# Output units of a fused attention and MoE block ordered by column halves, its LayerNorm's last step moved off VectorE

## The chip, the cores and the metric

The kernel runs on one core of a Trainium2 chip. The metric is the device time of one launch in microseconds (us), lower is better; three runs of a kernel give a median. Engines are named TensorE (PE), VectorE (DVE), ScalarE (ACT), GpSimd (POOL) and SyncE (SP), whose queue issues the large transfers.

## What is computed

One encoder block over 512 tokens of width 1024 in fp32: two attention mixers (a sliding window one and a sparse one), a gated merge, the projection `w_out`, a LayerNorm, a routed mixture of experts, a second LayerNorm.

```python
m = sigmoid(ga) * (oa @ w_branch_a) + sigmoid(gb) * (ob @ w_branch_b)
h = layernorm(ALPHA * x + m @ w_out, ln1_g, ln1_b)      # (x - mean) * rstd * g + b
# router: top-1 of 4 groups, then top-2 of its 8 experts, per token
y = sum over chosen experts of ((silu(h @ w_gate) * (h @ w_up)) * weight) @ w_down
out = layernorm(ALPHA * h + y, ln2_g, ln2_b)
```

## The kernel before

The program is written out by hand for each engine, with semaphores between them; the order in a block's text is the order on that engine. Tokens are four tiles of 128 (`TT` = 4). The stages are the input projections and attention, the branch products, the out stage, the expert loop and the tail. The change touches the out stage and how it hands over to the expert loop.

**Out stage.** `m @ w_out` is split in high and low parts, three matmuls for each of 8 row blocks `k`. A unit `("out", i)` is one token tile times one half of the 1024 columns: 24 matmuls into one PSUM bank (`bank_of`, L126). Before, unit `2t + h` is tile `t`, half `h`, so a tile's two halves follow each other. DVE takes a unit out of PSUM with `residual(t, h)` (L1766), which adds it to the scaled input rows in `h1` and sums the row; `centre(t)` (L1776) makes the mean and writes `z = (h1 - mean) * g`; ACT makes the sum of squares (`squares`, L1504), POOL the variance and `rstd` (L761, L764); `norm1(t)` (L1790) writes `h1 = z * rstd + b`, again on DVE, in two halves with the columns reordered (`row_half`, `in_half`), and signals `h1_ready`.

PE turns `z` (`turn_z`, L1082), ACT copies it to `h1T` (`copy_h1t`, L1511), PE multiplies by the router weights (`router`, L1093), DVE finds group and experts (`select`, L1799, and `weigh`, L1823), PE counts ranks in each expert (`rank`, L1104), and DVE makes the selection of rows from these (`place`, L1833). PE's order around this is L1143 to L1163, DVE's is L1855 to L1865:

```python
for t in range(TT):                # DVE before
    residual(t, 0)
    if t:
        select(t - 1); weigh(t - 1); place(t - 1)
    residual(t, 1); centre(t); norm1(t)
select(TT - 1); place(TT - 1)
```

After the last unit PE gathers the rows of experts 0 and 1 by matmul with the selection (`picked_rows`, L1115), makes the table of tokens of every expert (L1168), turns the picked rows (L1130), and starts expert 0. The rows of later experts are gathered from `h1_dram` by POOL (L772, L782), which waits until all four tiles of `h1` are stored there by SP (L626).

**Expert loop.** 32 experts of 3 MB of weights each (gate, up, down: 1 MB each, L564, L568, L581) pass through six slots of SBUF (`EXS`, `ex_off`). Per expert PE does L1229 (gate and up), L1211, L1130 and L1245 (down). A slot's gate and up are loaded again when PE is done with them (`refill_gate_up`, L634, waits `gu_done`; `refill_down`, L639, waits `d_done`). Slots 3, 4 and 5 lie over memory that the out stage still reads: slot 3's gate and up are the left columns of `w_o_lo`, slot 5 reaches into the merged input. So SP (L610 to L632) loads slots 0 to 2 before the out units, and the other 9 MB as the out stage lets go of its memory. SP issues in order: a wait for `h1_ready` ahead of a load holds that load too.

## Time and profile before

| | us |
|---|---|
| median of 3 runs (lowest, highest) | 757.41 (757.24, 758.32) |
| the profiled execution | 759.57 |
| its span, first to last instruction | 757.8 |
| PE busy | 731.0 (96%) |
| DVE, ACT, POOL busy | 376.3, 303.5, 255.4 |
| DMA over the span | 161.00 MB, 212 GB/s |

All times inside the kernel are counted from the span's start. The page's strip of 40 slices has about 19 us each; a line of the timeline gives start, duration, engine, source line, operation, output and inputs, a count where equal neighbours are merged, and in brackets the engine's idle time before it with the one that ended it. The out stage runs from 436.8 to 490, the hand-over to 503.2, the expert loop to 730.6.

### The profile page before, as it was taken

What the parts mean: (1) busy time and instruction counts of PE and PEld (TensorE: products, weight loads), DVE (VectorE), ACT (ScalarE), POOL (GpSimd) and SP (SyncE); (2) the same over time, 40 slices, a digit from 0 to 9 for tenths busy, and PEclk for the clock granted to TensorE, in tenths of its full rate; (3) what the DMA queues carried; (4) which work ended last, traced back from release to release, by engine and by line L of the source; (5) the groups of instructions that cost most, each with busy time, mean ns of one, the idle gap of its engine ahead of it and who ended that gap; (6) DMA issues with size and microseconds to landing.
All of it is one profiled execution on the core that took longest, in us unless ns stands there. A gap on an engine that the chain in (4) does not pass through costs nothing.

```text
span 757.8 us, 12102 instructions
## 1 busy us (share of the span) xinstructions
PE 731.0 (96%) x4400; PEld 511.3 (67%) x4400; DVE 376.3 (50%) x1001; ACT 303.5 (40%) x614; POOL 255.4 (34%) x310
## 2 busy tenths in 40 slices
PE   7999999999999999999999999999999999997894
PEld 6965886777777777778888878754555555554442
DVE  2436998877678867664222256645511111111146
ACT  5346325777556665565232141223322222221123
POOL 4721542222222222225695200023323333333211
PEclk9999999999999999999999999999999999999998
DMA  8511242222222222224631384699999999999973
GB/s 234 168 56 56 86 138 70 70 71 70 70 70 70 70 70 70 70 70 167 222 110 63 134 360 195 231 402 413 417 413 418 417 417 417 417 416 418 412 300 155
DMA packets 60199, 161.00 MB, mean 212 GB/s; under 512 B 8666, under 2 KB 37346, under 8 KB 48116
## 3 DMA queue, kind: packets, MB, share of 16 engines
q1 hardware_dynamic: 55108, 152.31, 53.4%
q0 software_dynamic: 5040, 8.02, 2.9%
q8 instruction: 31, 0.51, 0.3%
q14 instruction: 20, 0.16, 0.1%
HBM read 152.56 MB, written 16.25 MB: 223 GB/s over the span
## 4 chain that ended last, share of the span: by engine, by line
PE 85%; DMA 6%; DVE 3%; ACT 2%; issue 2%; POOL 1%; SPq 1%; DVEq 0%; POOLq 0%; ACTq 0%
PE psum L924 38%; PE psum L1229 12%; PE psum L1245 6%; PE psum L910 6%; PE psum L999 4%; DMA arena<-in_w_up_dram 4%; PE psum L1057 3%; PE psum L1130 2%; PE psum L1035 2%; PE psum L1051 2%; PE psum L852 1%; PE psum L969 1%; PE psum L1211 1%; DMA arena<-pair_rows 1%; PE psum L1100 1%
## 5 line engine op out<-in xcount | busy, mean ns | idle before, releaser
L924 PE MATMUL psum<-arena,arena 128*128 128x512 f32 (+1 forms) x1296 | 315.1, 394 | 0.2 <-POOL arena L709 0.2
L924 PEld LDWEIGHTS psum<-arena,arena 128*128 128x128 f32 x1296 | 235.6, 188 | 58.9 <-issue 14.1
L709 POOL TENSOR_TENSOR arena<-arena,arena 128x256 fp32r<-128x256 f32 (+1 forms) x138 | 138.1, 1035 | 234.3 <-ACT arena L1339 234.3
L1229 PE MATMUL psum<-arena,gate_a_T 128*64 128x256 f32 x1024 | 123.4, 383 | 6.9 <-DMA arena<-in_w_up_dram 6.7
L1229 PEld LDWEIGHTS psum<-arena,gate_a_T 128*64 128x64 f32 x1024 | 70.8, 137 | 55.0 <-issue 25.8
L1339 ACT ACTIVATE arena<-arena 128x2048 fp32r<-128x2048 f32 x27 | 51.5, 1907 | 37.1 <-DMA arena<-in_w_branch_b_dram 24.9
L1995 DVE COPY gate_a_T<-psum 128x128 f32<-128x128 f32 x32 | 9.3, 291 | 114.3 <-PE psum L1211 114.3
L1442 ACT ACTIVATE arena<-psum 128x1024 f32<-128x1024 f32 (+3 forms) x48 | 37.1, 773 | 67.6 <-PE psum L1035 48.4
L1432 ACT ACTIVATE arena<-arena,negm 128x193 f32<-128x193 f32 (+5 forms) x128 | 62.4, 492 | 3.6 <-DVE negm L1700 3.6
L1245 PE MATMUL psum<-arena,gate_a_T 128*64 128x512 f32 x256 | 61.9, 604 | 0.4 <-DVE gate_a_T L1995 0.4
L1550 ACT ACTIVATE gate_a_T<-psum 64x256 f32<-64x256 f32 x32 | 12.1, 377 | 117.5 <-PE psum L1229 117.5
L1989 DVE SCALAR_TENSOR_TENSOR gate_a_T<-gate_a_T,psum 64x256 f32<-64x256 f32 x32 | 13.3, 415 | 58.5 <-ACT gate_a_T L1550 58.3
L1699 DVE TENSOR_REDUCE mx<-arena 128x4 f32<-128x772 f32 (+5 forms) x48 | 40.5, 843 | 1.6
L1710 DVE TENSOR_SCALAR arena<-arena,mx 128x192 f32<-128x192 f32 (+4 forms) x128 | 40.3, 368 | 1.7
L794 POOL DMA_INDIRECT pair_rows<-gate_a_T,idx x30 | 30.9, 1029 | 30.3 <-ACT gate_a_T L1561 30.3
L910 PE MATMUL psum<-arena,arena 128*128 128x512 f32 x128 | 40.5, 398 | 0.4 <-DVE merged_low L1740 0.4
L782 POOL DMA_INDIRECT arena<-h_rows,idx x30 | 31.5, 1049 | 25.6 <-POOL idx L779 25.6
L1695 DVE SCALAR_TENSOR_TENSOR arena<-arena,psum 128x128 f32<-128x128 f32 (+3 forms) x64 | 28.2, 482 | 21.3 <-PE psum L999 21.3
L779 POOL COPY idx<-tok_i 128x1 int32 (+1 forms) x30 | 5.6, 185 | 85.8 <-PE psum L1130 85.8
L1561 ACT ACTIVATE gate_a_T<-psum 128x512 f32<-128x512 f32 x30 | 17.9, 597 | 39.4 <-PE psum L1245 39.4
L999 PE MATMUL psum<-arena,arena 64*128 64x192 f32 (+4 forms) x256 | 33.3, 389 | 0.0
L1245 PEld LDWEIGHTS psum<-arena,gate_a_T 128*64 128x64 f32 x256 | 15.7, 136 | 22.5 <-issue 18.2
(258 smaller groups left out, 881.9 us busy)
## 6 DMA issues: line engine op xcount, KB each, us to landing
arena<-in_w_down_dram SPq DMA_DIRECT2D x32, 1024.0 KB, 20.8
arena<-in_w_gate_dram SPq DMA_DIRECT2D x31, 1024.0 KB, 13.6
arena<-in_w_up_dram SPq DMA_DIRECT2D x31, 1024.0 KB, 17.7
arena<-in_w_in_dram SPq DMA_DIRECT2D x19, 1024.0 KB, 5.5
pair_rows<-arena SPq DMA_DIRECT2D x16, 256.0 KB, 5.7
arena<-in_w_branch_a_dram SPq DMA_DIRECT2D x4, 1024.0 KB, 5.8
arena<-in_w_branch_b_dram SPq DMA_DIRECT2D x4, 1024.0 KB, 5.2
arena<-in_w_out_dram SPq DMA_DIRECT2D x4, 1024.0 KB, 8.1
```

Of the source, the lines that this page charges most:

```text
L709: nc.gpsimd.tensor_tensor(lo[:, k], raw[:, k], hi[:, k], ALU.subtract).then_inc(w_split, DT // n)
L782: pool.indirect_dma_start(out=xg[s], out_offset=None, in_=h1_dram, in_offset=bass.IndirectOffsetOnAxis(ap=idx[:, s:s + 1], axis=0), bounds ...
L910: ins = nc.tensor.matmul(ps, mp, wp, start=k == 0 and p == 0, stop=k == DT - 1 and p == 2)
L924: ins = nc.tensor.matmul(ps[:, columns(kind)], wp[:, k, col:col + P], xp[:, k, columns(kind)], start=k == 0 and p == 0, stop=k == DT - 1 a ...
L999: ins = nc.tensor.matmul(psum[:, 2 * (n % 2) + par, 256 * i:256 * i + w], q, k, start=True, stop=True)
L1229: ins = nc.tensor.matmul(psum[CAP * g:CAP * g + CAP, 2 + s % 2, 0:FF], xgT[s % 2][:, k % 4, k // 4, :], ex_gu[slot][:, g, k, :], start=k = ...
L1245: ins = nc.tensor.matmul(psum[CAP * half:CAP * half + CAP, 4 + s % 2, :], hidT[s % 2][:, k, :], ex_d[slot][:, k, 512 * half:512 * half + 5 ...
L1339: nc.scalar.activation(w_hi[c % RING], w_raw[c % RING], ACT.Copy).then_inc(w_high, 1)
L1432: ins = nc.scalar.activation(out, src, ACT.Exp, bias=negm[:, n % 4, h:h + 1], accum_out=den[:, n % 4, h:h + 1])
L1442: nc.scalar.activation(pt_sb[n % 2][:, 0:cols], psum[:, 4:6, :].rearrange("p b c -> p (b c)")[:, 0:cols], ACT.Copy).then_inc(pt_copied, 1)
L1699: step(V.tensor_reduce(mx[:, n % 4, 0:heads], s[:, :, w0:] if kind == "A" else s, AX.X, ALU.max))
L1710: ins = V.tensor_scalar(part, part, mx[:, n % 4, h:h + 1], None, ALU.mult)
```

## The change

1. **Order of the units.** Unit `TT * h + t` is tile `t`, half `h`: the four left halves come first, then the four right halves. The last one shares bank 4 with the first right half. `residual` of the left half of tile 3 is taken late (`TAKEN_IN`), since its `h1` rows lie over merged input that unit 6 still reads.
2. **SP.** Once the four left halves are done, slot 3's gate and up and slot 4's down are loaded. Then come the stores of `h1` tiles 0, 1 and 2, each behind its `h1_ready`; then, behind `wo_front_read` and the last unit, the 5 MB of slot 3's down, slot 5 and slot 4's gate; then the store of tile 3 and slot 4's up.
3. **LayerNorm's last step.** `norm1` is gone from DVE. ACT does `h1 = z * rstd` in two instructions behind the copies of `h1T` (`scale_z`), and POOL adds `b` in two instructions (128x512 each) before it signals `h1_ready`. `centre(t)` waits for `z_scaled` and no longer for `h1_ready`.
4. **PE and DVE order.** `rank(t)` comes a tile later; `router(2)` stands behind the last unit; `place(2)` stands behind `select(3)`, and `rank(2)` has a bank of its own.

```diff
@@ -90,7 +90,7 @@
         out += [("b", 2 * i + j, 21 + 2 * i, 128 * j) for j in range(2)]
-    out += [("out", 2 * t + i, None, 512 * i) for t in range(TT) for i in range(2)]
+    out += [("out", TT * i + t, None, 512 * i) for i in range(2) for t in range(TT)]
     return out
@@ -118,6 +118,9 @@
+TAKEN_IN = [0, 1, 2, 4, 5, 6, 3, 7]
+
+
 def columns(kind):
@@ -126,7 +129,7 @@
     if kind == "out":
-        return 4 + i % 4
+        return 4 if i == 2 * TT - 1 else 4 + i % TT
     if kind in "ab":
@@ -424,6 +427,7 @@
+        RANK_BANK = [3, 3, 6, 3]
@@ -473,8 +477,8 @@
             elif kind == "out":
-                if UNITS[u][1] >= 4:
-                    eng.wait_ge(r_ready, UNITS[u][1] - 3)
+                if UNITS[u][1] >= TT:
+                    eng.wait_ge(r_ready, TAKEN_IN.index(UNITS[before[-1]][1]) + 1)
             elif before:
@@ -611,25 +615,28 @@
             expert(2, 2)
+            sp.wait_ge(unit_done, UNIT["out", TT - 1] + 1)
+            gate_up(3, 3)
+            down(4, 4)
             for t in range(TT):
-                if t == TT - 2:
-                    sp.wait_ge(unit_done, UNIT["out", 2 * t + 1] + 1)
-                    residual_rows(TT - 1)
                 if t == TT - 1:
-                    sp.wait_ge(unit_done, UNIT["out", 6] + 1)
-                    gate_up(3, 3)
-                    down(4, 4)
-                    sp.wait_ge(unit_done, UNIT["out", 7] + 1)
+                    sp.wait_ge(wo_front_read, 1)
+                    down(3, 3)
+                    up(5, 5)
+                    sp.wait_ge(unit_done, UNIT["out", 2 * TT - 1] + 1)
                     gate(4, 4)
-                    down(3, 3)
+                    gate(5, 5)
+                    down(5, 5)
                 sp.wait_ge(h1_ready, t + 1)
...
                              ).then_inc(h1_stored, 16)
+                if t == TT - 3:
+                    sp.wait_ge(unit_done, UNIT["out", 2 * TT - 2] + 1)
+                    residual_rows(TT - 1)
             for rows, row in ((ln2g, ln2_g), (ln2b, ln2_b)):
...
             up(4, 4)
-            expert(5, 5)
@@ -763,6 +770,11 @@
                                         ).then_inc(rstd_ready, 1)
+                pool.wait_ge(z_scaled, 2 * t + 2)
+                for h in range(2):
+                    rows = row_half(h1[:, t, :], h)
+                    ins = nc.gpsimd.tensor_tensor(rows, rows, in_half(ln1b, h), ALU.add)
+                ins.then_inc(h1_ready, 1)
             pool.wait_ge(h1_stored, 16 * TT)
@@ -893,7 +905,7 @@
                 if kind == "out":
-                    t = i // 2
+                    t = i % TT
                     tok = slice(t * P, (t + 1) * P)
@@ -908,6 +920,8 @@
                             ins = nc.tensor.matmul(ps, mp, wp, start=k == 0 and p == 0, stop=k == DT - 1 and p == 2)
+                        if i == 2 * TT - 1 and k == DT // 2 - 1:
+                            ins.then_inc(wo_front_read, 1)
                     if k1 == DT:
@@ -1104,18 +1118,20 @@
-                if t:
-                    pe.wait_ge(ranks_taken, t)
+                if t == TT - 2:
+                    pe.wait_ge(r_ready, TAKEN_IN.index(2 * TT - 2) + 1)
+                elif t:
+                    pe.wait_ge(ranks_taken, min(t, TT - 2))
                 for v in range(t + 1):
                     pe.wait_ge(oh_ready, v + 1)
-                    ins = nc.tensor.matmul(psum[:, 3, 0:NE], (upper_h if v == t else ones_h)[:, :],
+                    ins = nc.tensor.matmul(psum[:, RANK_BANK[t], 0:NE], (upper_h if v == t else ones_h)[:, :],
                                            oh_both[:, v, :], start=v == 0, stop=v == t)
...
                 if t == 0:
-                    pe.wait_ge(r_ready, 5 + e)
+                    pe.wait_ge(r_ready, TAKEN_IN.index(2 * TT - 1 if e == 0 else TT + e) + 1)
                 pe.wait_ge(h1_ready, t + 1)
@@ -1142,24 +1158,28 @@
             for k0, k1 in ((0, BACK), (BACK, DT)):
-                for h in range(2):
-                    unit(UNIT["out", h], k0, k1)
+                for t in range(2):
+                    unit(UNIT["out", t], k0, k1)
+            for u in range(2, TT + 1):
+                unit(UNIT["out", u])
             for t in range(1, TT):
-                unit(UNIT["out", 2 * t], 0, 4)
+                u = UNIT["out", TT + t]
+                unit(u, 0, 4)
                 turn_z(t - 1)
-                unit(UNIT["out", 2 * t], 4, DT)
+                unit(u, 4, 6)
+                if t >= 2:
+                    rank(t - 2)
+                unit(u, 6, DT)
                 router(t - 1)
-                unit(UNIT["out", 2 * t + 1], 0, 6)
-                rank(t - 1)
-                unit(UNIT["out", 2 * t + 1], 6, DT)
+            turn_z(TT - 1)
             picked_rows(0, 0)
+            router(TT - 1)
             picked_rows(0, 1)
-            turn_z(TT - 1)
-            router(TT - 1)
-            picked_rows(0, 2)
+            rank(TT - 2)
             picked_rows(1, 0)
...
             picked_rows(1, 1)
+            picked_rows(0, 2)
             picked_rows(0, TT - 1)
@@ -1517,11 +1537,19 @@
+            def scale_z(t):
+
+                act.wait_ge(rstd_ready, t + 1)
+                for h in range(2):
+                    nc.scalar.activation(row_half(h1[:, t, :], h), in_half(z, h), ACT.Copy, scale=ln[:, 0, 4, t:t + 1]
+                                         ).then_inc(z_scaled, 1)
+
             for t in range(TT):
...
                 copy_h1t(t)
+                scale_z(t)
                 if t == TT - 2:
@@ -1765,7 +1793,7 @@
-                u = UNIT["out", 2 * t + h]
+                u = UNIT["out", TT * h + t]
                 cols = slice(h * D // 2, (h + 1) * D // 2)
@@ -1775,26 +1803,17 @@
-                dve.wait_ge(r_ready, 2 * t + 2)
+                dve.wait_ge(r_ready, TAKEN_IN.index(TT + t) + 1)
                 V.tensor_scalar(ln[:, 0, 1, t:t + 1], ln[:, 0, 0, t:t + 1], ln[:, 0, 5, t:t + 1], -1.0 / D, ALU.add,
...
                     dve.wait_ge(h1t_done, 2 * t)
-                    dve.wait_ge(h1_ready, t)
+                    dve.wait_ge(z_scaled, 2 * t)
                 for h in range(2):
...
                                            ALU.add, ALU.mult).then_inc(z_ready, 1)
-
-            def norm1(t):
-
-                dve.wait_ge(rstd_ready, t + 1)
-                dve.wait_ge(z_ready, 2 * t + 2)
-                for h in range(2):
-                    ins = V.scalar_tensor_tensor(row_half(h1[:, t, :], h), in_half(z, h), ln[:, 0, 4, t:t + 1],
-                                                 in_half(ln1b, h), ALU.mult, ALU.add)
-                ins.then_inc(h1_ready, 1)
@@ -1834,7 +1853,7 @@
                 dve.wait_ge(ranked, t + 1)
-                rank = psum[:, 3, 0:NE]
+                rank = psum[:, RANK_BANK[t], 0:NE]
                 step(V.scalar_tensor_tensor(sel_code[:, t, :], rank[:, 0:PEX], 1.0, oh_both[:, t, 0:PEX], ALU.add,
@@ -1852,16 +1871,20 @@
             step(V.tensor_scalar(dst_shift[:, :], tokid[:, 0:1], CAP + 0.5, -1.0, ALU.is_gt, ALU.add))
+            for t in range(TT - 1):
+                residual(t, 0)
             for t in range(TT):
-                residual(t, 0)
+                if t == TT - 1:
+                    residual(t, 0)
+                residual(t, 1)
+                centre(t)
                 if t:
...
                     weigh(t - 1)
+                if 0 < t < TT - 1:
                     place(t - 1)
-                residual(t, 1)
-                centre(t)
-                norm1(t)
             select(TT - 1)
+            place(TT - 2)
             place(TT - 1)
```


**DVE, from the last residual to the table of tokens.** `arena_105` is `h1`, `arena_107` is `z`; `L1773`/`L1801` residual, `L1787`/`L1815` centre, `L1795` norm1, `L1804`/`L1823` the first instruction of `select`, `L1829`/`L1848` the last of `weigh`, `L1838`/`L1857` to `L1847`/`L1866` `place`, `L1870`/`L1893` behind the table. Before:

```order
L1773 SCALAR_TENSOR_TENSOR arena_105,ln<-psum,arena_105 128x512
L1779 TENSOR_SCALAR ln<-ln 128x1
L1787 SCALAR_TENSOR_TENSOR arena_107<-arena_105,ln,arena_94 128x512 x2
L1795 SCALAR_TENSOR_TENSOR arena_105<-arena_107,ln,arena_95 128x512 x2
L1804 SCALAR_TENSOR_TENSOR strip<-psum,ln,const 128x40
...
L1821 TENSOR_SCALAR arena_150<-arena_148,dst_code 128x2x32
L1838 SCALAR_TENSOR_TENSOR sel_code<-psum,arena_149 128x2
...
L1847 TENSOR_TENSOR in_slot<-col_s,ranks 128x2x64
L1870 TENSOR_SCALAR strip<-psum 128x32
```

With the change:

```order
L1801 SCALAR_TENSOR_TENSOR arena_105,ln<-psum,arena_105 128x512 x2
L1807 TENSOR_SCALAR ln<-ln 128x1
L1815 SCALAR_TENSOR_TENSOR arena_107<-arena_105,ln,arena_94 128x512 x2
L1823 SCALAR_TENSOR_TENSOR strip<-psum,ln,const 128x40
...
L1848 TENSOR_TENSOR md<-best 128x1
L1823 SCALAR_TENSOR_TENSOR strip<-psum,ln,const 128x40
...
L1857 SCALAR_TENSOR_TENSOR sel_code<-psum,arena_149 128x2
...
L1866 TENSOR_TENSOR in_slot<-col_s,ranks 128x2x64
L1857 SCALAR_TENSOR_TENSOR sel_code<-psum,arena_149 128x2
...
L1866 TENSOR_TENSOR in_slot<-col_s,ranks 128x2x64
L1893 TENSOR_SCALAR strip<-psum 128x32
```

The two instructions of norm1 are gone; a whole `select` and `weigh` (of tile 2) and a whole `place` now stand between the last residual and the table, beside those of tile 3.

**PE, from the last out unit to the table** (`L1122`/`L1138` picked rows, `L1089`/`L1103` turn_z, `L1100`/`L1114` router, `L1111`/`L1127` rank, `L1168`/`L1188` the table, `L1130`/`L1146` turning the rows). Before:

```order
L1122 MATMUL psum<-arena_105,arena_158 64x512 x4
L1089 MATMUL psum<-ident,arena_107 128x128 x8
L1100 MATMUL psum<-rw,arena_106 128x40 x8
L1122 MATMUL psum<-arena_105,arena_158 64x512 x4
L1111 MATMUL psum<-arena_149,ones_h 128x32 x3
L1111 MATMUL psum<-arena_149,upper_h 128x32
L1122 MATMUL psum<-arena_105,arena_158 64x512 x4
L1168 MATMUL psum<-arena_150,in_slot 64x32 x16
L1130 MATMUL psum<-ident,arena_108 128x128 x4
L1122 MATMUL psum<-arena_105,arena_158 64x512 x4
```

With the change (its first two rows follow the last matmul of the last unit):

```order
L1114 MATMUL psum<-rw,arena_106 128x40 x8
L1103 MATMUL psum<-ident,arena_107 128x128 x8
L1138 MATMUL psum<-arena_105,arena_158 64x512 x2
L1114 MATMUL psum<-rw,arena_106 128x40 x8
L1138 MATMUL psum<-arena_105,arena_158 64x512 x2
L1127 MATMUL psum<-arena_149,ones_h 128x32 x2
L1127 MATMUL psum<-arena_149,upper_h 128x32
L1138 MATMUL psum<-arena_105,arena_158 64x512 x2
L1127 MATMUL psum<-arena_149,ones_h 128x32 x3
L1127 MATMUL psum<-arena_149,upper_h 128x32
L1138 MATMUL psum<-arena_105,arena_158 64x512 x6
L1188 MATMUL psum<-arena_150,in_slot 64x32 x16
```

A second router product has come behind the last unit and ahead of turn_z; two picked rows (a pair is two matmuls) stand on either side of the router, and the third for expert 0 now follows the last rank.

**SP's queue, from the first store of `h1`** (`h_rows<-arena_105`; arena_114, 115, 116 are gate and up of slots 3, 4, 5, arena_120, 121, 122 down of slots 3, 4, 5). Before:

```order
L626 DMA h_rows<-arena_105 128x1024 x2
L605 DMA arena_105<-in_x_dram 128x1024
L626 DMA h_rows<-arena_105 128x1024
L564 DMA arena_114<-in_w_gate_dram 128x2048
L568 DMA arena_114<-in_w_up_dram 128x2048
L581 DMA arena_121<-in_w_down_dram 128x2048
L564 DMA arena_115<-in_w_gate_dram 128x2048
L581 DMA arena_120<-in_w_down_dram 128x2048
L626 DMA h_rows<-arena_105 128x1024
L629 DMA arena_94<-in_ln_g_dram 1x1024
L629 DMA arena_95<-in_ln_b_dram 1x1024
L568 DMA arena_115<-in_w_up_dram 128x2048
```

With the change:

```order
L568 DMA arena_114<-in_w_gate_dram 128x2048
L572 DMA arena_114<-in_w_up_dram 128x2048
L585 DMA arena_121<-in_w_down_dram 128x2048
L631 DMA h_rows<-arena_105 128x1024 x2
L609 DMA arena_105<-in_x_dram 128x1024
L631 DMA h_rows<-arena_105 128x1024
L585 DMA arena_120<-in_w_down_dram 128x2048
L572 DMA arena_116<-in_w_up_dram 128x2048
L568 DMA arena_115<-in_w_gate_dram 128x2048
L568 DMA arena_116<-in_w_gate_dram 128x2048
L585 DMA arena_122<-in_w_down_dram 128x2048
L631 DMA h_rows<-arena_105 128x1024
```

Three loads now stand ahead of the stores, and five loads stand between the stores of tiles 2 and 3.

## Rows read from the trace of the kernel before

**Rows 1.** The page's strip of 40 slices: DMA busy tenths, and GB/s.
```profile
DMA  8511242222222222224631384699999999999973
GB/s 234 168 56 56 86 138 70 70 71 70 70 70 70 70 70 70 70 70 167 222 110 63 134 360 195 231 402 413 417 413 418 417 417 417 417 416 418 412 300 155
```
**Rows 2.** What PE waited for, 500 to 730 us: total, times, longest.
```profile
PE psum L1229 <- DMA arena<-in_w_up_dram: 6.7, 5, 1.6
```
**Rows 3.** Windows: length, busy time of PE, PEld, DVE, ACT, POOL, PE clock, DMA share, GB/s.
```profile
465.00:479.00 14.00, 14.00 (x77) 11.76 (x76) 8.81 (x35) 2.33 (x4) 0.87 (x4) 1.00 0.20 75
...
500.00:520.00 20.00, 19.49 (x171) 11.78 (x169) 8.89 (x34) 5.22 (x12) 5.90 (x8) 1.00 1.01 415
...
700.00:720.00 20.00, 17.64 (x129) 9.55 (x126) 2.55 (x7) 3.43 (x7) 5.76 (x9) 1.00 1.02 413
```
**Rows 4.** Timeline of SP's queue: first of the late loads, last, first refill.
```profile
482.63 0.33 SPq L564 DMA_DIRECT2D arena<-in_w_gate_dram  x1
...
498.04 0.52 SPq L581 DMA_DIRECT2D arena<-in_w_down_dram  x1
506.83 0.33 SPq L564 DMA_DIRECT2D arena<-in_w_gate_dram  x1
```
**Rows 5.** Packets of SP's queue, 482.6 to 506.83 us: count, MB, share of engines.
```profile
q1 hardware_dynamic: 1363, 9.18, 98.6%
```
**Rows 6.** POOL's gathers: the page's queue line, and the first gather's instruction.
```profile
q0 software_dynamic: 5040, 8.02, 2.9%
```
```profile
502.49 1.30 POOL L772 DMA_INDIRECT arena<-h_rows,tok_i  x1 [9.21 <-DMA h_rows<-arena]
```
**Rows 7.** Windows behind the load issued at 436.95, DMA idle before: last column GB/s.
```profile
437.00:437.50 0.50, 0.50 (x4) 0.42 (x3) 0.50 (x1) 0.50 (x2) 0.00 (x0) 1.00 0.00 0
437.50:438.00 0.50, 0.50 (x4) 0.32 (x2) 0.50 (x2) 0.50 (x2) 0.00 (x0) 1.00 0.81 115
...
439.00:439.50 0.50, 0.50 (x4) 0.41 (x3) 0.50 (x2) 0.50 (x2) 0.00 (x0) 1.00 1.01 426
```
**Rows 8.** Timeline of PE: router of tile 2, last unit, what follows, expert 0.
```profile
482.44 1.87 PE L1100 MATMUL psum<-rw,arena 128*128 128x40 f32 x16
484.14 0.71 PE L910 MATMUL psum<-arena,arena 128*128 128x512 f32 x2
...
489.99 1.94 PE L1122 MATMUL psum<-arena,arena 128*64 128x512 f32 x8
...
503.16 3.62 PE L1229 MATMUL psum<-arena,gate_a_T 128*64 128x256 f32 x32
```
**Rows 9.** Timeline of DVE: select, weigh, place of tile 2; residual to place of tile 3.
```profile
484.35 0.26 DVE L1804 SCALAR_TENSOR_TENSOR strip<-psum,ln,const 128x40 f32<-128x40 f32 x1 [0.94 <-PE psum L1100]
...
487.75 0.15 DVE L1829 TENSOR_TENSOR md<-best 128x1 f32<-128x1 f32 x1
488.72 0.16 DVE L1838 SCALAR_TENSOR_TENSOR sel_code<-psum,arena 128x2 f32<-128x2 f32 x1 [0.81 <-PE psum L1111]
...
490.09 0.69 DVE L1773 SCALAR_TENSOR_TENSOR arena<-psum,arena 128x512 f32<-128x512 f32 x1
...
491.08 1.42 DVE L1787 SCALAR_TENSOR_TENSOR arena<-arena,ln,arena 128x512 f32<-128x512 f32 x2
...
495.37 0.26 DVE L1804 SCALAR_TENSOR_TENSOR strip<-psum,ln,const 128x40 f32<-128x40 f32 x1 [0.64 <-PE psum L1100]
...
499.38 0.29 DVE L1847 TENSOR_TENSOR in_slot<-col_s,ranks 128x128 f16<-128x128 f32 x1
```
**Rows 10.** Groups by form: an ACT copy of 128x512 inside SBUF.
```profile
L1458 ACT ACTIVATE arena<-arena 128x512 fp32r<-128x512 f32 x16 | 9.2, 618 | 0.0
```
**Rows 11.** Timelines: two POOL instructions of 128x1024, and a DVE one beside them.
```profile
384.61 4.77 POOL L750 TENSOR_TENSOR arena<-arena,arena 128x1024 fp32r<-128x1024 f32 x2
```
```profile
388.72 1.21 DVE L1755 TENSOR_TENSOR gate_a_T<-gate_a_T,arena 128x512 f32<-128x512 f32 x1
```
**Rows 12.** One line's instructions: durations in ns, least, median, most.
```profile
L1755 DVE TENSOR_TENSOR gate_a_T<-gate_a_T,arena x8: 684/799/1205, 367.0 to 438.8; 128x512 f32<-128x512 f32 x8
```
```profile
L1700 DVE TENSOR_SCALAR negm<-mx x48: 168/170/735, 112.5 to 335.4; 128x2 f32<-128x2 f32 x32, 128x4 f32<-128x4 f32 x16
```
```profile
L704 POOL TENSOR_TENSOR arena<-arena,arena x1: 3362/3362/3362, 19.1 to 19.1; 128x1024 fp32r<-128x1024 f32 x1
```

4 lines of the change are left out of this document (2 added, 2 removed).

## The prediction

> **What bounds the kernel now.** I read the strip of 40 slices first. The DMA moves 412 to 418 GB/s in nearly every slice from the 27th to the 38th, and only 70 in most slices of the first half [rows 1]. So the expert loop looks bound by its transfers, although PE is busy 96% of the span. The waits say the same: from 500 to 730 us PE waits for weights only five times, 6.7 us in all [rows 2], and the windows show the DMA full at both ends of the loop, while it is nearly idle at 465 to 479 us [rows 3]. PE starts the loop with six slots full of weights and is ahead of the transfers until it has used them up; then it takes a weight when it lands. From there on the end depends on one thing: when the unbroken stream of refills began.
>
> The queue's timeline gives that moment. SP issues the late loads from 482.63 to 498.04, and the first refill at 506.83, when PE has finished expert 0's gate and up [rows 4]. The late loads are 9 MB of weights (9 x 1.049 = 9.44) and a store (0.52), 9.96 MB; SP's queue had moved 9.18 of it by 506.83 [rows 5]. So 0.78 MB was left, and 0.26 MB of two gathers (8.02 MB in 63 of them, 0.13 each, the first issued at 502.49 [rows 6]): 1.04 MB, which at 417 GB/s is 2.5 us. The refills' bytes began at about 509.3, with no gap before them. How much of the cover a gap would need follows from a load issued while the DMA was idle: issued at 436.95, nothing moved before 437.5, 115 GB/s then, and the full rate only at 439.0 [rows 7]. Against full flow that is about 1.6 us lost (estimate, from these windows).
>
> The Trainium skill (DMA: Bandwidth & Descriptors, "Anatomy of one DMA — SWDGE (gpsimd) path") puts most of the fixed 2 us at the end of a transfer, in the receipt of the write, so almost nothing would be lost at the start. The rows differ for this queue; by the page the stream would begin at 511.2, and the sum below would come to 759.3 in place of 760.9.
>
> **What sets the start of expert 0.** It starts at 503.16. PE ends the last unit with router(2) ahead of it: router 482.44 to 484.14, unit to 489.99 [rows 8]. On DVE, tile 2's select and weigh take 484.35 to 487.90, its place 488.72 to 490.09 (1.37); then come residual(3,1), z from 491.08 to 492.50, select(3) at 495.37, and the last place ends at 499.67 [rows 9]. The table of tokens and the turned rows follow on PE. So the chain after the out units is DVE's, and whatever is put into it moves the start.
>
> **The change, part by part.**
>
> 1. *Units by halves, router(2) behind the last unit.* The last unit ends 1.7 us earlier, near 488.2. DVE cannot use all of it: between the rank that comes 18 matmuls into that unit (about 1.4 us before its end) and residual(3,1) it now does place(1), 1.37, and residual(3,0), 0.7. residual(3,1) starts near 489.0, 1.1 earlier, and z ends near 491.4.
>
> 2. *What stands behind it.* Before, tile 2's select, weigh and place were done ahead of residual(3,1). Now select(2) and weigh(2) (487.90 - 484.35 = 3.55) come behind z(3): to 494.95. select(3) takes 495.37 to 499.67 less its place of 1.37, so some 3.0: to 498.0. Then place(2) and place(3), 1.37 each: 500.7 against 499.67, +1.0. One more pair of picked rows behind the last rank: 0.2 (eight 128x512 matmuls took 1.94 [rows 8]; two at 0.24 stand there more, half of it beside DVE). Without anything on POOL, expert 0 starts **1.2 later**. Taking norm1 off DVE gives the chain nothing at tile 3: before, two of it (1.4 us) lay in the wait between z's end at 492.50 and select's start at 495.37 while PE turned z. At tiles 0 to 2 DVE waits for PE's units anyway.
>
> 3. *ACT.* Two scalings a tile, as long as the copy of 128x512 inside SBUF, 0.62 [rows 10], behind the copies of h1T, which PE's router reads. It lies beside PE: nothing. If it came ahead, it would cost the router 1.2.
>
> 4. *POOL.* Two adds of 128x512 a tile. Two adds of 128x1024 took 4.77, so one here is about 1.2 and a pair 2.4. A DVE instruction beside them, with two inputs in SBUF, took 1.21 where the same line mostly takes 0.8 [rows 11, 12]; a tiny one (two elements a row) that mostly takes 0.17 took 0.74 once [rows 12]. Both look like an instruction that waits until POOL's ends. Tile 2's pair falls beside place(1) and the residuals, tile 3's beside select(2), weigh(2) and select(3): both on the chain. A pair costs DVE between 0 (it only meets the residuals, which read PSUM) and 2.4 (DVE stands still for all of it). I take 1.6, two thirds, since the chain there is mostly of small instructions with SBUF inputs but some get in between: +3.2 for two pairs. Tiles 0 and 1 have their pairs under the units: nothing.
>
> The Trainium skill (SBUF — State Buffer, "Who interferes with whom") says that GpSimd and VectorE share a pair of ports as an exclusive lock: a VectorE operation with two SBUF inputs, or in a two-port mode, stands still until the other's instruction is over. The two rows agree in kind. By that rule both pairs would be lost whole, 4.9 in place of 3.2, and the time would be 762.6.
>
> So expert 0 starts 4.4 us later (bounds 1.2 and 6.1), near 507.6.
>
> 5. *SP.* Three loads go out about 20 us earlier, near 461, into a time when the DMA is idle [rows 3]. The other five stand behind the stores of h1, each of which waits for its `h1_ready`; that of tile 2 comes only when POOL has added, near 490.0 (z(2) turned by 485.4, copies and scalings 2.4, adds 2.4). So 0.52 + 5.24 + 0.52 + 1.05 = 7.3 MB go out from 491.6 on and land by 509.4 at 417 GB/s. That is ahead of the first refill, now at 506.83 + 4.4 = 511.2, whose bytes flow at 512.8. The DMA stands idle for some 3 us that it did not before. The refill stream begins 512.8 - 509.3 = **3.5 us later**, and so does every weight behind it. The 3 MB that came early buy nothing, because the slots are full and no further load may go out until PE frees one. PE's waits at the end get shorter by the difference: 6.7 + 3.5 - 4.4 = 5.8.
>
> **The sum.** 759.57 + 3.5 = 763.1 for the profiled execution. That one stood 2.2 above the median of 757.41, so the median comes to **760.9**. A measurement of this kernel can tell about 0.2%, 1.5 us, from no change.
>
> **The rivals.**
>
> - *No contention.* POOL's adds meet only residuals and waits. The start is 1.2 later, the refill is issued at 508.0 and flows at 509.6, just behind the prefill's 509.4: the stream moves by 0.3, and up to 0.7 with some blocking. Time 757.7 to 758.1, taken as 757.9. For it: most durations of L1755 are at its median. Against: its longest and L1700's. Chance 0.22.
> - *The early loads pay (the other side).* If the loop's end hangs on how many bytes are in SBUF when PE starts, and the refill is not the gate, then 3 MB more in hand take away all five waits, 6.7, and PE's own pace sets the end: 757.4 - 6.7 + 1.2 = 751.9. It decides if the queue behind the first refill was more than 2.5 us long, which rows 5 speak against: what the early loads relieve is only that backlog. Chance 0.09.
> - *POOL is slower.* The adds read `b` in reordered columns. The one 128x1024 instruction at the start of the kernel took 3.36 [rows 12], 1.7 for half. Two pairs that block in full are 6.8, the start moves 8.0 and the stream 7.1: 764.5. Chance 0.13.
> - That the change doesn't do what it says: the early loads may not go out early. They stand ahead of every `h1_ready` wait now, and depend on the fourth left unit alone, so I give this no chance of its own; since they buy nothing, the sum would be the same unless the five late ones were later still.
>
> **The numbers.** Forecast 0.56, the others as above. The range goes from 757.2 (no contention, less half a microsecond for the medians) to 764.0, which takes in the forecast's upper bound of 762.6 and the part of the slow case with a little less blocking. Below it lies the second rival, above it most of the third. Faster by over 0.2% 0.09, within it 0.22 (the first rival), slower 0.69.
>
> **What would show it.** Last unit ending near 488.2; place(3) ending near 504 and expert 0 at 507.6; DVE instructions of select, weigh or place several times their usual length beside POOL's adds of 1.2; three loads issued near 461 and five near 490; DMA near idle from 470 to 490 and for about 3 us ahead of a first refill at 511; PE's waits for weights 5.8 in all. The prediction is wrong if the first refill is issued later and the end does not move with it, or if DVE is not held up by POOL, or if the chain after the last unit is not DVE's: a wait of PE for `h1_ready` of tile 3 would show that.

## The result, and the profile after

| us | before | changed |
|---|---|---|
| median (lowest, highest), 7 runs each | 757.64 (757.24, 758.86) | 760.56 (759.43, 761.65) |
| profiled execution, its span | 759.57, 757.8 | 761.18, 759.3 |
| PE busy | 731.0 | 734.7 |
| POOL, ACT busy | 255.4, 303.5 | 266.4, 308.6 |

The changed kernel is slower: ratio 1.0036, 95% interval 1.0024 to 1.0047, 2.9 us between the medians. The forecast was 760.9.

**Where the two traces line up.** The spans differ by only 1.5 us where the medians differ by 2.9, since the profiled execution of before is 1.9 above its median and that of the changed kernel 0.6. Part of this may lie at its start, where the clock of before's trace was low (mean clock 0.994; 45 of the 59 executions of before beside the experiments have 0.996 or 0.997). From the windows of before, PE clock in the third column from the right:

```profile
8.00:10.00 2.00, 1.67 (x8) 1.47 (x8) 0.00 (x0) 0.61 (x2) 0.00 (x0) 0.62 1.00 346
10.00:12.00 2.00, 1.56 (x5) 1.21 (x5) 0.69 (x1) 1.02 (x2) 0.82 (x1) 0.52 1.07 390
```

It is not the whole of it: the changed kernel's trace comes to the out stage 0.3 later still. So from here on places are also counted from the out stage's first matmul: 436.76 in before, 437.08 in the changed kernel, written as +66.4 and the like. And how late the transfers run is taken from their bytes: what the DMA moved in the 285 us from that matmul on. Before and changed:

```profile
DMA packets 19525, 110.01 MB, mean 386 GB/s; under 512 B 4345, under 2 KB 4345, under 8 KB 7631
```
```profile
DMA packets 19269, 108.82 MB, mean 382 GB/s; under 512 B 4293, under 2 KB 4293, under 8 KB 7466
```

1.19 MB less, at 0.417 MB a us, is a stream **2.9 us late**, as much as the medians differ. A second measure is the place of the last expert's down product, which follows the last weights:

```profile
728.70 1.94 PE L1245 MATMUL psum<-arena,gate_a_T 128*64 128x512 f32 x8 [0.40 <-DVE gate_a_T L1995]
```
```profile
730.40 1.94 PE L1265 MATMUL psum<-arena,gate_a_T 128*64 128x512 f32 x8 [0.41 <-DVE gate_a_T L2018]
```

That is +291.94 and +293.32, **1.4 us late** only. Why the two measures differ by 1.4 is not known; twelve of the thirteen kernels compared with this one trace of before show a difference of 0.9 to 1.8, so a good part of it is likely to be that trace's own. The time itself is read from the medians; the places in a trace say where it is lost, to about a microsecond.

The strip of slices and the waits of PE from 500 to 730 us in the changed kernel, against [rows 1] and [rows 2]:

```profile
DMA  8511242222222222224632397399999999999984
GB/s 235 166 56 55 87 138 70 70 71 70 70 70 70 70 70 70 70 70 167 222 110 73 123 375 294 126 366 413 400 409 419 416 418 417 417 416 418 412 319 174
```
```profile
PE psum L1249 <- DMA arena<-in_w_up_dram: 4.8, 4, 1.5
...
PE psum L1146 <- DMA arena<-h_rows,tok_i: 0.9, 1, 0.9
```

The early loads show in the 25th slice (294 for 195), the hole before the late ones in the 26th (126 for 231). PE waits less for weights, and has a new wait: for the gathered rows of expert 2.

SP's queue, against [rows 4]:

```profile
459.95 0.33 SPq L568 DMA_DIRECT2D arena<-in_w_gate_dram  x1
...
490.09 0.32 SPq L631 DMA_DIRECT2D h_rows<-arena  x1
490.46 0.43 SPq L585 DMA_DIRECT2D arena<-in_w_down_dram  x1
...
497.66 0.33 SPq L631 DMA_DIRECT2D h_rows<-arena  x1
...
509.79 0.35 SPq L568 DMA_DIRECT2D arena<-in_w_gate_dram  x1
```

The late loads and the first refill go out as forecast in kind, and the windows around that refill show the gap (before had 412 GB/s over all of 506 to 512):

```profile
510.00:511.00 1.00, 1.00 (x24) 0.88 (x22) 0.66 (x2) 0.71 (x2) 0.69 (x2) 1.00 0.52 74
511.00:512.00 1.00, 0.82 (x9) 0.70 (x10) 0.17 (x1) 0.06 (x1) 0.70 (x2) 1.00 0.62 205
```

PE behind the last unit, against [rows 8]:

```profile
488.18 1.87 PE L1114 MATMUL psum<-rw,arena 128*128 128x40 f32 x16
491.25 1.95 PE L1103 MATMUL psum<-ident,arena 128*128 128x128 f32 x8 [1.20 <-DVE arena L1815]
493.13 1.85 PE L1138 MATMUL psum<-arena,arena 128*64 128x512 f32 x4
494.91 1.98 PE L1114 MATMUL psum<-rw,arena 128*128 128x40 f32 x16
...
506.12 3.62 PE L1249 MATMUL psum<-arena,gate_a_T 128*64 128x256 f32 x32
```

and the windows of the same stretch:

```profile
490.00:491.00 1.00, 0.05 (x1) 0.00 (x0) 0.93 (x4) 0.50 (x1) 0.07 (x1) 1.00 0.12 49
491.00:492.00 1.00, 0.75 (x4) 0.75 (x5) 1.00 (x3) 0.74 (x2) 0.17 (x1) 0.65 1.12 401
492.00:493.00 1.00, 1.00 (x6) 0.80 (x4) 0.83 (x7) 0.56 (x1) 0.57 (x2) 0.50 0.96 246
493.00:494.00 1.00, 1.00 (x3) 0.30 (x4) 0.86 (x7) 0.80 (x3) 0.00 (x0) 0.50 1.00 352
494.00:495.00 1.00, 1.00 (x5) 0.10 (x1) 0.90 (x6) 1.00 (x2) 0.00 (x0) 0.64 0.94 385
```

PE stood idle for 1.2 us, waiting for z of tile 3, and then ran at half rate (1.2 GHz for 2.4) for some 3.4 us. Four records of picked rows (two matmuls of the program, which leave two records each) took 1.85 there and 1.08 at full clock. The other executions of the changed kernel have a mean clock of 0.990 to 0.995, where before mostly has 0.996 or 0.997; a stretch of 3.4 us at half rate is 0.002 of the mean (estimate), so most of them are likely to have one.

DVE, against [rows 9]:

```profile
488.05 0.88 DVE L1866 TENSOR_TENSOR in_slot<-col_s,ranks 128x128 f16<-128x128 f32 x1
...
490.44 1.42 DVE L1815 SCALAR_TENSOR_TENSOR arena<-arena,ln,arena 128x512 f32<-128x512 f32 x2
...
495.17 1.26 DVE L1848 TENSOR_TENSOR md<-best 128x1 f32<-128x1 f32 x1
497.09 0.26 DVE L1823 SCALAR_TENSOR_TENSOR strip<-psum,ln,const 128x40 f32<-128x40 f32 x1 [0.67 <-PE psum L1114]
...
502.35 0.29 DVE L1866 TENSOR_TENSOR in_slot<-col_s,ranks 128x128 f16<-128x128 f32 x1
```

Counted from the out stage's first matmul, the start of expert 0 came from +66.40 to +69.04. Its pieces, each from start to start unless said:

| piece | before | changed | difference |
|---|---|---|---|
| first matmul to z(3) | 54.32 | 53.36 | -0.96 |
| z(3) to select(3) | 4.29 | 6.65 | +2.36 |
| select(3) to the last place's end | 4.30 | 5.55 | +1.25 |
| to expert 0 | 3.49 | 3.48 | 0 |

From place(1) on, two DVE instructions were held up by POOL's adds: 0.88 for 0.29, and 1.26 for 0.15. The second cost nothing: select(3) behind it waited for PE's router anyway. POOL's adds took 1.26 to 1.32 each.

The change's order of work does not always run so. Two of the kernels below, e3_all_late and e8_split_refill, have the same program on PE and DVE up to expert 0 and differ from it in their loads. In their traces PE waited the same 1.19 us for z and its clock stayed at 1.00; two instructions of weigh(2) were held, 1.32 for 0.24 and 1.33 for 0.37, and DVE went into select(3) without a wait; then PE waited 2.04 for its rank, the clock fell behind that, and expert 0 started at +70.5. From e8_split_refill:

```profile
489.84 1.32 PE L1106 MATMUL psum<-ident,arena 128*128 128x128 f32 x8 [1.19 <-DVE arena L1822]
```
```profile
493.07 1.32 DVE L1847 TENSOR_SCALAR arena<-arena,dst_code 128x64 f16<-128x64 f16 x1
494.43 1.33 DVE L1852 TENSOR_SCALAR arena<-arena,dst_code 128x32 f16<-128x32 f16 x2
```

So a start read from one trace of this order stands for itself to about 1.5 us.

### The profile page after: what moved, and what is told of

It reads as the page before. It is cut to its first block, busy times and chain, and to the rows that moved or that the text cites. A ratio compares the mean times of both kernels' runs of the same rounds, so it can differ in the third digit from the quotient of the medians.

```text
span 759.3 us, 12105 instructions
## 1 busy us (share of the span) xinstructions
PE 734.7 (97%) x4400; PEld 513.9 (68%) x4400; DVE 375.2 (49%) x993; ACT 308.6 (41%) x622; POOL 266.4 (35%) x318
## 4 chain that ended last, share of the span: by engine, by line
PE 80%; DMA 9%; SPq 3%; DVE 3%; issue 2%; POOL 2%; ACT 2%; DVEq 0%; POOLq 0%
PE psum L938 38%; PE psum L1249 10%; PE psum L922 5%; PE psum L1265 5%; PE psum L1013 4%; DMA arena<-in_w_up_dram 4%; PE psum L1071 3%; PE psum L1049 2%; PE psum L1146 2%; PE psum L1065 2%; PE psum L864 1%; DMA h_rows<-arena 1%; PE psum L983 1%; DMA arena<-pair_rows 1%; PE psum L1231 1%
## 5 line engine op out<-in xcount | busy, mean ns | idle before, releaser
L1462 ACT ACTIVATE arena<-psum 128x1024 f32<-128x1024 f32 (+3 forms) x48 | 37.2, 775 | 67.5 <-PE psum L1049 48.4
L1265 PE MATMUL psum<-arena,gate_a_T 128*64 128x512 f32 x256 | 61.9, 604 | 0.4 <-DVE gate_a_T L2018 0.4
L1578 ACT ACTIVATE gate_a_T<-psum 64x256 f32<-64x256 f32 x32 | 12.1, 378 | 115.4 <-PE psum L1249 115.4
```

Source lines behind the costliest of these rows:

```text
L1265: ins = nc.tensor.matmul(psum[CAP * half:CAP * half + CAP, 4 + s % 2, :], hidT[s % 2][:, k, :], ex_d[slot][:, k, 512 * half:512 * half + 5 ...
L1462: nc.scalar.activation(pt_sb[n % 2][:, 0:cols], psum[:, 4:6, :].rearrange("p b c -> p (b c)")[:, 0:cols], ACT.Copy).then_inc(pt_copied, 1)
```

## The experiments

Each kernel ran 5 to 12 times beside runs of before on the same chip. "Start" is the start of expert 0 from the out stage's first matmul; "late" is how late the stream of transfers runs against the trace of before, from the bytes of 285 us as above; "loop end" is the place of the last expert's down product, less before's +291.94; "time" is median less median of before in the same job, with the 95% interval that the ratio gives.

| kernel | start | late | loop end | time |
|---|---|---|---|---|
| before | +66.4 | 0 | 0 | 0 |
| changed | +69.0 | 2.9 | 1.4 | +2.9 (1.8 to 3.6) |
| e1_cover | +69.5 | 2.8 | 1.7 | +2.7 (1.8 to 4.1) |
| e2_delay | +71.5 | 4.7 | 3.1 | +4.9 (4.0 to 6.4) |
| e3_all_late | +70.5 | 11.6 | 9.9 | +12.1 (10.3 to 13.0) |
| e4_ln_split | +67.5 | 2.6 | 2.2 | +2.2 (1.4 to 3.2) |
| e5_norm_dve | +72.0 | 5.2 | 3.8 | +5.5 (5.0 to 6.8) |
| e6_loads_ahead | +68.9 | 2.0 | 1.1 | +1.9 (1.4 to 3.1) |
| e7_order | +69.3 | 4.3 | 2.6 | +3.3 (2.7 to 4.7) |
| e8_split_refill | +70.5 | 4.8 | 3.8 | +3.4 (2.3 to 4.9) |
| e9_store_first | +69.1 | 2.3 | 1.1 | +2.3 (1.3 to 3.4) |
| e10_no_add | +68.7 | 2.1 | 1.0 | +0.9 (0 to 1.6) |
| e11_fill | +69.4 | 2.6 | 1.3 | +1.5 (1.1 to 2.3) |
| e12_split_ahead | +67.6 | 1.9 | 0.7 | +1.2 (1.0 to 2.3) |

Start and time do not go strictly together: e11_fill starts later than the changed kernel and loses less, and e10_no_add starts only 0.3 earlier and loses 2.0 less. Other gates than the start are told below.

**e1_cover.**

```diff
-            turn_z(TT - 1)
+            picked_rows(1, 0)
+            picked_rows(1, 1)
+            turn_z(TT - 1)
```
(and the same two calls taken out further down)

> The changed kernel with expert 1's picked rows of tiles 0 and 1 (four matmuls, 1.0 us, no dependence on tile 3) moved ahead of turn_z(3), into the 1.2 us in which PE waited there for z. Nothing else is changed. Theory A (the granted clock): in the changed kernel PE's clock fell from 1.00 to 0.50 right behind that idle 1.2 us, and turn_z, picked rows and router ran at half rate there, 1.7 us in all; with the gap filled the clock stays at 1.00, select(3) starts near 496.3 in place of 497.09 (DVE's weigh(2), held up by POOL, is the next limit), expert 0 starts near 505.2 in place of 506.12, and the time falls by about 0.9 us against the changed kernel. Theory B (contention of POOL and DVE alone sets the later start): DVE's chain is untouched, no difference, 0. Theory C (the gap of the DMA ahead of the first refill comes from the order of SP's loads, not from PE): 0.

The gap was filled, the clock stayed at 1.00 there, and select(3) started at +59.3 in place of +60.0, as expected. But the picked rows were then missing while DVE did select(3): PE stood idle for 1.90 and 0.95 us, the clock fell at 498.8, and table and rows ran at half rate:

```profile
498.33 3.27 PE L1138 MATMUL psum<-arena,arena 128*64 128x512 f32 x8 [0.95 <-DVE arena L1860]
```

The same eight records take 1.94 at full clock. The start and the time stayed. The clock is a real part of the loss where it falls, but moving idle time elsewhere moves the fall with it.

**e2_delay.** 12 more matmuls in before:

```diff
-            picked_rows(1, TT - 1)
+            picked_rows(1, TT - 1, signal=False)
+            for t in range(2):
+                picked_rows(1, t, alone=True)
+            for t in range(TT):
+                picked_rows(1, t)
```

> The kernel before with 12 matmuls of 64x512 added ahead of expert 0 (expert 1's picked rows made once more and a half), 2.9 us at 0.243 each: expert 0 starts 2.9 us later, near 506.1, as it does in the changed kernel; loads, units and LayerNorm as before. Theory A (the end follows the first refill, which has 0.9 us of slack, 2.5 of backlog less 1.6 of latency): 2.9 - 0.9 = +2.0 us against before, with a gap of some 2 us in the DMA ahead of the first refill, and PE's waits for weights at the end 0.9 shorter. Theory B (a loop bound by its transfers absorbs a later start, and the changed kernel's loss comes from its loads): 0. Theory C (every microsecond of the start counts in full): +2.9.

The delay was mis-sized: a matmul of the program is two records in the trace, so 24 records, and the start moved by 5.1 us, not 2.9. The time moved by 4.9 (4.0 to 6.4), the stream by 4.7. Absorption (theory B) is out. The slack is 0.4 us by the stream and 2.0 by the loop's end, and the interval of the time holds the forecast's 0.9 and zero as well: it is not measured closer than that. A loop that is full of transfers still pays for a later start, since its first refill waits for it. The gap around the refill (issued at 511.77):

```profile
510.00:511.00 1.00, 1.00 (x13) 0.66 (x10) 0.00 (x0) 0.00 (x0) 0.00 (x0) 1.00 0.20 82
511.00:512.00 1.00, 1.00 (x10) 0.54 (x7) 0.00 (x0) 0.22 (x1) 0.00 (x0) 1.00 0.00 0
512.00:513.00 1.00, 1.00 (x24) 0.87 (x22) 0.67 (x2) 0.71 (x2) 0.00 (x0) 1.00 0.29 33
513.00:514.00 1.00, 0.82 (x9) 0.71 (x10) 0.16 (x1) 0.04 (x1) 0.82 (x1) 1.00 0.63 229
```

**e3_all_late.**

```diff
-            sp.wait_ge(unit_done, UNIT["out", TT - 1] + 1)
-            gate_up(3, 3)
-            down(4, 4)
...
                     sp.wait_ge(wo_front_read, 1)
+                    gate_up(3, 3)
+                    down(4, 4)
```

> The changed kernel with the three early loads (slot 3's gate and up, slot 4's down) issued with the other late ones, behind the store of h1 tile 1, so that all 9 MB go out from about 488 to 490 on. Theory A (the stream of refills begins at the later of two moments, the landing of all the late loads and the first refill's issue plus 1.6): 0.52 MB of the store and 9.44 of loads from 490 to 491.6 on and then the store of tile 3 come to 10.5 MB, 25.1 us at 417 GB/s, 516.0 to 516.7 against 511.4 in the changed kernel: +4.6 to +5.3 us, and no gap in the DMA; the three early loads then do pay in the changed kernel, as what keeps the loads off the path. Theory B (early loads buy nothing at all, since the slots are full either way when PE starts): 0.

(The loads stand behind the store of tile 2, counted from 0, and not of tile 1.) It was twice as bad as expected, +12.1. The gathers are the likely cause that the theory lacked: tile 3's store lands only behind all 8 loads, POOL's gathers wait for it, and PE for their rows:

```profile
521.56 1.10 PE L1145 MATMUL psum<-ident,arena 128*128 128x128 f32 x4 [6.37 <-DMA arena<-h_rows,tok_i]
```

By its bytes the stream was 7.3 late at +90, about what the theory gave, and 11.6 at +150; the wait of 6.4 us for rows ends at +86, ahead of that second loss. So a second gate stands beside the first refill: the store of the last tile of `h1`. And the early loads do pay, as what keeps the late ones short.

**e4_ln_split.** In before (DVE; `scale_z` on ACT and the adds on POOL are added word for word as in the change):

```diff
                 centre(t)
-                norm1(t)
```

> The kernel before (its order of units, its loads, its PE and DVE order) with only the LayerNorm's last step moved as in the change: two scalings on ACT, two adds on POOL. Theory A (contention matters little here): only instructions with SBUF inputs that meet an add are held up, by 0.6 to 1.1 us each and once or twice on the chain; select(3) waits for PE's router at 495.37 anyway, and norm1(3) is gone from DVE there; expert 0 starts 0 to +0.9 later and the time is within 0.9 of before: 0 (-0.3 to +0.9). Theory B (contention is what the change costs): two pairs of adds block DVE for 1.6 each or more, expert 0 starts 3 us later and the time is +2.3 us.

The time is theory B's (+2.3), but the start moved by only 1.1 where that theory needs 3. The contention is there, once, in select(3):

```profile
493.90 2.49 POOL L769 TENSOR_TENSOR arena<-arena,arena 128x512 f32<-128x512 f32 x2 [1.85 <-ACT arena L1529]
```
```profile
495.23 1.21 DVE L1814 TENSOR_TENSOR strip<-strip 128x32 f32<-128x32 f32 x1
```

It is 1.0 of the start's 1.1. But the late loads began 2.1 later too (+48.0 for +45.9): SP waits for `h1_ready(2)` ahead of them, and the store behind that signal went out 3.4 later than in before (+47.6 for +44.2). There was no gap at the refill, so the late loads set the stream.

**e12_split_ahead.** e4 with the three loads ahead of that wait:

```diff
                     residual_rows(TT - 1)
-                if t == TT - 1:
                     sp.wait_ge(unit_done, UNIT["out", 6] + 1)
                     gate_up(3, 3)
                     down(4, 4)
+                if t == TT - 1:
```

> The kernel of e4_ln_split (before with only LayerNorm's last step split) with the first three late loads ahead of SP's wait for h1_ready(2), at the end of unit 6 as in before. In e4_ln_split h1_ready(2) came 2.2 us later than in before and held those loads for 2.1 us, and the stream of transfers, which has no gap there, ran 2.6 us late, though expert 0 started only 1.1 later. Theory A (with a queue that never runs dry, the stream is set by when the late loads begin; else by the first refill plus 2.4): the loads begin on time, the refill at +1.1 then decides, the stream is 1.0 us late: -1.6 against e4_ln_split, +0.6 to +1.2 against before. Theory B (the loss of e4_ln_split is contention or the start of expert 0): 0 against e4_ln_split.

The stream gained 0.75 us and the time 1.0 against e4, of 1.6 expected: in the direction of theory A, with the intervals of the two kernels (1.0 to 2.3 and 1.4 to 3.2) overlapping. Its account of the rest does not hold: the stream was 1.9 late and not 1.0, with no gap at the refill. The last four loads stand behind tile 3's store and with it behind its `h1_ready`; they went out from +61.9 on, +59.0 in before, and the queue ran low around them (363 GB/s in the same window of before):

```profile
498.00:500.00 2.00, 1.88 (x24) 0.72 (x20) 1.15 (x7) 0.44 (x1) 0.00 (x0) 1.00 0.74 238
```

**e5_norm_dve.** In the changed kernel (DVE; `scale_z` and POOL's adds are taken out):

```diff
                 centre(t)
+                norm1(t)
                 if t:
```

> The changed kernel with LayerNorm's last step back on DVE (norm1 as before, right behind z); order of units, loads, PE and the rest as in the change. Theory A (the DVE chain is full: per tile it now has residual, z, select, weigh and place, 7.2 us, in the 8.3 us that PE takes for a tile, and the four last pieces stand behind the last unit): 1.4 us more on it at each tile, less its idle 0.6 at each; z(3) comes 0.5 to 1 later, norm1(3) stands ahead of select(2); expert 0 starts 1 to 3 us later and the time is 1 to 3 us above the changed kernel's, +4 to +6 against before. Theory B (contention with POOL is what the change costs, 3.2 us on the chain): without it the time is 0 to 2 us below the changed kernel's.

Theory A: +5.5 against before, 2.6 above the changed kernel; the start moved by 3.0. In this order of units DVE's chain is full, and taking `norm1` off it is worth more than what the adds on POOL cost. (PE waited 1.48 for z here, and its clock fell behind that too.)

**e6_loads_ahead.**

```diff
-                if t == TT - 1:
+                if t == TT - 2:
                     sp.wait_ge(wo_front_read, 1)
```

> The changed kernel with the five late loads issued ahead of the store of h1 tile 2, so behind the last unit (51 us after the out stage's first matmul) and no longer behind h1_ready(2) (53 us). Theory A (the stream of refills begins when the first refill is issued, plus the time until its bytes flow; the prefill has landed by then either way): the DMA only stands idle some 2 us longer ahead of the first refill: 0 (within 0.5) against the changed kernel. Theory B (the late loads' start sets the stream): -2 us.

+1.9 against the changed kernel's +2.9, where 0 was expected and -2 by theory B; the intervals overlap (1.4 to 3.1, 1.8 to 3.6). The start was 0.2 earlier and the wait for expert 2's rows (0.9) was gone, since tile 3's store lay behind fewer bytes.

**e7_order.** e1 and these, on PE and DVE:

```diff
-            router(TT - 1)
+            router(TT - 1, between=TT - 2)
             picked_rows(0, 1)
-            rank(TT - 2)
-            rank(TT - 1)
             picked_rows(0, 2)
+            picked_rows(1, 2)
+            rank(TT - 1)
...
-                if 0 < t < TT - 1:
+                if 0 < t:
                     place(t - 1)
             select(TT - 1)
-            place(TT - 2)
```
(`between` puts that tile's rank into the middle of the router; the later call of the picked rows (1, 2) is taken out)

> The changed kernel with another order on PE and DVE behind the last unit, nothing added or left out: expert 1's picked rows of tiles 0 and 1 ahead of turn_z(3), rank(2) in the middle of router(3), place(2) ahead of select(3) on DVE, and the picked rows of tile 2 for both experts ahead of rank(3), so that PE has work during select(3). Theory A (PE's clock halves behind an idle microsecond, and place(2) behind select(3) is on the chain): the clock stays at 1.00 from 486 to 510, place(2)'s 1.2 us leave the chain in part, and 1.0 us of picked rows go from behind the table: expert 0 starts 1.5 to 3 us earlier than in the changed kernel, and the time falls by as much, to +0 to +1.4 against before. Theory B (the start of expert 0 does not set the end): 0 against the changed kernel.

Wrong on the start: +69.3. place(2) now lay beside the adds, and two instructions there took 1.25 for 0.22 and 1.05 for 0.42; the clock fell as well, at 501.7. And the wait for expert 2's rows grew to 2.2 us. The stream lost 4.3.

**e8_split_refill.** PE counts `wo_front_read` up to 2 behind expert 0's fourth row block, and waits for `wo_landed` (96) where it next reads slot 0; on SP:

```diff
-            refill_gate_up(0, 0)
+            sp.wait_ge(wo_front_read, 2)
+            gate_up_part(EXS, 0, 0, DT // 2, wo_landed)
+            sp.wait_ge(gu_done, 1)
+            gate_up_part(EXS, 0, DT // 2, DT, gu_landed[0])
```

> The changed kernel with the first refill in two parts: the rows of gate and up that expert 0 reads first (k below 4, 1 MB) are loaded again when it is half way through them, 1.8 us earlier, the rest when it is done, as before. The start of expert 0 and everything ahead of it stay. Theory A (the DMA stands idle until the first refill's bytes come, and every later byte moves with them): the gap in the DMA is 1.8 us shorter and the time falls by 1.8 us against the changed kernel, to +1.1 against before. Theory B (what counts is when PE starts the loop, its pace and its clock): 0.

No gain. In the trace that is shown the start was 1.5 later than in the changed kernel, as told above, so the first half went out only 0.2 earlier; but the windows suggest why an earlier first half would not pay alone: the gap comes back ahead of the next refill (515.72), which waits for expert 1.

```profile
509.00:511.00 2.00, 2.00 (x33) 1.45 (x28) 0.54 (x2) 0.80 (x2) 1.59 (x2) 1.00 0.90 242
511.00:513.00 2.00, 1.82 (x21) 1.31 (x18) 0.29 (x1) 0.18 (x1) 1.70 (x2) 1.00 0.76 201
513.00:515.00 2.00, 2.00 (x20) 1.30 (x18) 1.21 (x5) 0.00 (x0) 0.01 (x1) 1.00 0.83 275
```

Theory A was too simple: PE's pace over the first two refills counts, and not only the first one's issue.

**e9_store_first.**

```diff
                     gate(4, 4)
-                    gate(5, 5)
-                    down(5, 5)
...
+            gate(5, 5)
+            down(5, 5)
             sp.wait_ge(routed, TT)
             up(4, 4)
```

> The changed kernel with two of the five late loads (slot 5's gate and down) moved behind the store of h1 tile 3 in SP's queue. In the changed kernel that store is issued at 497.66 behind 5.2 MB and lands 10.4 us later; POOL's gathers wait for it, and PE waited 0.9 us for the gathered rows of expert 2. Theory A (two gates: the first refill, and these rows, which hold back expert 2 and with it the later refills): the store lands some 5 us earlier, the wait of 0.9 is gone; the first refill is issued as before and its bytes flow 2.4 us later as before, so the stream gains at most that 0.9: 0 to -0.9 against the changed kernel. Theory B (the store's delay costs nothing): 0, with the 0.9 gone from PE's waits and come back as a wait for weights.

The wait for the rows is gone, and the stream gained 0.5, the time 0.6: inside theory A's range, and inside the intervals.

**e10_no_add.**

```diff
-                for h in range(2):
-                    rows = row_half(h1[:, t, :], h)
-                    ins = nc.gpsimd.tensor_tensor(rows, rows, in_half(ln1b, h), ALU.add)
-                ins.then_inc(h1_ready, 1)
+                nc.gpsimd.tensor_tensor(h1[:, t, 0:1], h1[:, t, 0:1], ln1b[:, 0:1], ALU.add).then_inc(h1_ready, 1)
```

> The changed kernel with POOL's two adds of b for a tile shrunk to one add of one column (b is left out of all other columns), so that POOL reads almost nothing of SBUF beside DVE; everything else stays, h1_ready comes some 2.3 us earlier. Theory A (contention costs 0.6 us at tile 2's place and up to 0.6 at tile 3's select, 1.2 in all, and a later tile 3's wait of PE is then short of the idle microsecond that lets the clock fall): expert 0 starts 0.6 to 1.5 us earlier and the time falls by as much. Theory B (contention was the 3.2 us of the forecast): -3 us.

This kernel leaves `b` out of all columns but the first, so its rows of `h1` lack `b`. place's last instruction took 0.29 again, z(3) started at +52.9 for +53.4, but the start moved by only 0.3. PE still stood idle (0.75), the clock still fell, and DVE waited 1.92 us for the router:

```profile
494.63 0.26 DVE L1820 SCALAR_TENSOR_TENSOR strip<-psum,ln,const 128x40 f32<-128x40 f32 x1 [1.92 <-PE psum L1111]
```

So without the contention PE's slow stretch sets the start, and without the slow stretch (e1, e3, e8) DVE does: the two stand side by side. The time is 2.0 below the changed kernel's, with intervals that do not meet, and the start explains 0.3 of that. The rest is not settled; with the adds gone, `h1_ready` and with it the loads and the last store come earlier too.

**e11_fill.** e7 with e9's queue, and (`fill(n)` is n matmuls of tile 0's rows into bank 7, the result unused):

```diff
             picked_rows(0, 1)
+            fill(1)
             picked_rows(0, 2)
             picked_rows(1, 2)
+            fill(2)
             rank(TT - 1)
+            fill(2)
```

> The kernel of e7_order with SP's order of e9_store_first and five filler matmuls (64x512 each, result unused) where PE waited 0.7, 1.0 and 1.0 us for DVE. Theory A: the clock stays at 1.00 from 486 to 510 (in e7_order it fell to 0.50 at 501.8 for 3.4 us, 1.7 us of work lost), expert 0 starts 1.2 to 1.7 us earlier than in e7_order, the wait for expert 2's rows (2.2 us) is gone: -2 to -3 us against e7_order, +0.5 to +1.3 against before. Theory B (the clock is no cost of the change; the chain is DVE's alone): 0 to -0.5 against e7_order from the fillers, and what the rows give.

The clock stayed at 1.00 throughout. The start did not move (+69.4): DVE's chain with its two held instructions is as long, and two fillers held rank(3) for some tenths. Of the 1.8 us gained on e7 the wait for the rows of expert 2 (2.2, now gone) is the only cause seen, and e9's change of the queue is in this kernel too. It starts 3.0 later than before and loses 1.5, less than the changed kernel, with intervals that overlap (1.1 to 2.3 and 1.8 to 3.6). Nothing tried beats before.

## Why the prediction was right, and where it was not

The time (760.9 for 760.56), the sign and the mechanism at the end held: the stream of refills begins with the first one's issue, a gap opens in front of it, and every weight behind it is late. It was forecast at 3.5 us and is 2.9 by the bytes. That it came so close is in part luck. The start was forecast 1.8 later than this trace has it (4.4 for 2.6), and about 1.0 us that is lost behind the first refill was not in the sum.

1. **Units by halves.** The last unit ended at +51.1 for +53.2, 2.1 earlier and not 1.7; that it stands at the forecast's 488.2 comes from the 0.3 between the two traces. z(3) was to be 1.1 earlier before any contention. It was 0.96 earlier with 0.6 of contention at place(1) in it, and 1.4 in e10, without the adds.
2. **place(2) behind select(3).** Its 1.37 measured 1.25 on the path. The 0.2 for picked rows took records for matmuls (a pair is four records, about 1 us); it cost nothing, beside DVE's last two places.
3. **Contention, the term that was too large in this trace.** 3.2 us on the chain for two pairs. Measured: 0.6 at place(1) on the chain, 1.1 at weigh(2) off it, and 1.0 in e4's select(3). In e3 and e8 the second pair cost weigh(2) 2.0, on the chain, so the forecast's 1.6 a pair lies inside what was seen and a pair costs 0.6 to 2.0. Each add catches one instruction at most, and often none, since much of select reads PSUM, reduces or replaces and passes beside the adds. The rule of the Trainium skill (SBUF — State Buffer, "Who interferes with whom") agrees with which instructions stood still (two SBUF inputs, or a small tensor_scalar), and not with what I worked out from it: both pairs lost whole, and that at 4.9 us where two pairs of 2.4 are 4.8.
4. **A step that failed in this trace: "the chain after the out units is DVE's".** From z(3) to select(3) the forecast's way, DVE's select(2) and weigh(2), gives 0.7 more than before and 2.3 with the second pair of adds. Measured were 2.36, by the other way: PE's turn_z at half rate, four records of picked rows now between turn_z and router, and the router. DVE was done 0.66 before it. So the size of this stretch was right by luck, and by DVE's way it would have been 0.66 shorter. The order that PE's picked rows came into was read and not priced, and the gap that router(2) leaves in front of turn_z was not asked for its effect on the clock. In e1, e3 and e8, where the clock stayed up there, DVE's way was the longer.
5. **The start.** 4.4 forecast, 2.6 measured in this trace, from items 1 to 4; 4.1 in e3 and e8 with the same order.
6. **Slack at the first refill, about right, and a loss behind it that was not in the sum.** The slack of 0.9 comes from 2.5 of backlog and a latency of 1.6. In the 3 us from that refill's issue before moved 1.22 MB and the changed kernel 0.60:

```profile
DMA packets 273, 1.22 MB, mean 406 GB/s; under 512 B 89, under 2 KB 89, under 8 KB 151
```
```profile
DMA packets 84, 0.60 MB, mean 199 GB/s; under 512 B 11, under 2 KB 11, under 8 KB 11
```

   0.62 MB is 1.5 us, and against full flow the changed kernel, e1, e2 and e6 lose 1.56, 1.34, 1.56 and 1.68: the forecast's 1.6. At that issue the changed kernel had moved 0.96 MB more than before, 2.3 us of the 2.5. So at the first refill the stream is 2.6 - 2.3 + 1.5 = 1.8 late. From there to the end of the 285 us the bytes fall behind by another 1.0. In e2, 0.7 of that loss stands 6 to 8 us behind the first refill's issue, around the second refill (517.59); in the changed kernel it is spread over the next 40 us. The queue then has no backlog to fall back on, so PE's pace over several refills is likely to be what it pays for; no kernel here tests that alone.
7. **A wait that was not in the sum.** The store of tile 3 now stands behind 5.2 MB and lands 10.4 us after its issue, 6.8 in before; PE waited 0.9 us for expert 2's rows. The prediction moved the loads past that store and asked only for the loads.
8. **"The 3 MB that came early buy nothing."** Right against before as far as the slots go, wrong for the changed kernel: without them it loses 9 us more (e3).
9. PE's waits for weights: 5.8 forecast; 4.8, and the 0.9 for rows.

The rival without contention is out by its time (757.9), and instructions were held; but e10, without the adds, still starts 2.3 later than before and not 1.2, so most of the later start is not contention. (Its prefill would land at 509.2 by its own terms, 491.6 and 7.3 MB, not 509.4.) The faster rival fell with e2 and with the gap. POOL's adds are 1.3, not 1.7.

What stays open: why the clock stays up behind 1.19 us of idle PE in e3 and e8 and falls behind 1.20 in the changed kernel; where the 2.0 us between e10 and the changed kernel come from; why e11 loses so little with so late a start; and the difference of 1.4 between the bytes and the loop's end.

## What to carry to other kernels

A stage that is bound by transfers with all its buffers full is still gated by the compute that frees the first one; a delay ahead of it is paid nearly in full once the queue has run dry by then (5.1 us of delay cost 4.9 here), so count the backlog in the queue at that issue, and what a gap costs beyond the wait, at the first refill and at the next ones. When work is regrouped so that one engine's steps bunch up at the end, follow the chain on every engine that is in it, with what fills each wait. When loads are moved in a queue, ask which small transfer now stands behind them and who waits for it.

## What the runs showed of the hardware

- PE's clock fell to half for about 3.4 us, 1.7 us of work lost, in every kernel with the changed order but e11: behind 1.20 us of idle (changed), 1.19 and 1.20 (e6, e9), 1.48 (e5), 0.75 (e10), 1.90 and 0.95 (e1), 0.96 and 0.95 (e7), 2.04 (e3 and e8). The length of one wait does not decide it: in e3 and e8 the clock stayed at 1.00 behind 1.19 us of idle at the very place where it fell in the changed kernel. It stayed in e11, where fillers covered the waits, and in e4 and e12 in spite of 1.59 us of idle:

```profile
497.73 0.19 PE L1116 MATMUL psum<-arena,upper_h 128*128 128x32 bf16 x1 [1.59 <-DVE arena L1821]
```

- A first refill into an idle DMA lost 1.3 to 1.7 us against full flow within 3 us of its issue (the changed kernel, e1, e2, e5, e6, e9, e10, e11; bytes as in point 6), as the one issue in before suggested. The Trainium skill's account (DMA: Bandwidth & Descriptors, "Anatomy of one DMA — SWDGE (gpsimd) path"), which puts most of the fixed time at the end, is for GpSimd's path; on SP's queue here the loss is in front: behind e2's refill, issued at 511.77, the DMA moved 33 GB/s from 512 to 513 and 229 from 513 to 514.
- A 0.15 us instruction on DVE (one element a row) took 1.26 beside an add on POOL.
